# A recurrent mixer whose gate branch runs one block behind its gates, with the gate products in three products of halves

## The reference

```python
def rglru_direction(xc, w_g, b_g, lam, h0, reverse):
    xb = xc.reshape(B, T, LRU_BLOCKS, LRU_BLOCK)              # 8 blocks of 128 channels
    g = jnp.einsum('btnk,gnkj->gbtnj', xb, w_g).reshape(2, B, T, D_RNN) + b_g[:, None, None, :]
    r, ig = jax.nn.sigmoid(g[0]), jax.nn.sigmoid(g[1])
    log_a = -LRU_C * r * jax.nn.softplus(-lam)
    a = jnp.exp(log_a)
    u = jnp.sqrt(-jnp.expm1(2.0 * log_a)) * (ig * xc)
    # h = a * h + u along the tokens, forwards or backwards
def rglru_mixer(...):
    z = h @ w_in                                              # 1024 x 2048
    g, xc = gelu(z[..., :D_RNN]), dwconv_centred(z[..., D_RNN:], conv_w, conv_b)
    y = forward(xc) + backward(xc)                            # two directions
    return (y * g) @ w_out
```

## Time and profile before

| what | value |
|---|---|
| median of 3 runs | 1773.4 us (1772.84 to 1774.81) |
| profiled execution, its own time | 1770.4 us |
| its span in the trace | 1768.7 us |
| mean granted PE clock | 0.985 of full speed |
| PE busy | 1640.8 us (93%) |
| DVE busy | 710.4 us (40%) |
| ACT busy | 553.3 us (31%) |
| POOL busy | 182.1 us (10%) |

### The profile page before, as it was taken

One profiled execution on the slowest core, in us unless ns is written; L12 is line 12 of the kernel. 1 busy time (PEld: TensorE's weight loads), 2 busy tenths in 40 slices (PEclk: granted clock), 3 DMA queues, 4 the chain that ended last, 5 costly groups with the idle time before them and its releaser, 6 DMA issues.

```text
span 1768.7 us, 23506 instructions
## 1 busy us (share of the span) xinstructions
PE 1640.8 (93%) x9838; PEld 876.1 (50%) x9838; DVE 710.4 (40%) x1432; ACT 553.3 (31%) x970; POOL 182.1 (10%) x203
## 2 busy tenths in 40 slices
PE   5999989889999999999989999999969998888887
PEld 3766767543333333333349888888733333222222
DVE  4667666621222122122136766765441222022213
ACT  5777883400111111111027656655300000000002
POOL 1000010010001001001001235433000000000001
PEclk8999999989999999999999999999979999999999
DMA  9555352699999999999993200023499999999996
GB/s 374 199 215 168 121 225 97 238 355 406 393 403 395 391 402 400 390 403 403 396 382 143 72 1 2 1 72 131 188 366 421 420 422 420 422 421 421 421 421 254
DMA packets 89593, 520.78 MB, mean 294 GB/s; under 512 B 11347, under 2 KB 19648, under 8 KB 33936
## 3 DMA queue, kind: packets, MB, share of 16 engines
q1 hardware_dynamic: 80128, 487.74, 68.3%
q0 software_dynamic: 9360, 31.54, 5.7%
HBM read 502.37 MB, written 16.88 MB: 294 GB/s over the span
## 4 chain that ended last, share of the span: by engine, by line
PE 59%; SPq 21%; ACT 7%; DVE 6%; DMA 5%; issue 2%; ACTq 0%; DVEq 0%; POOLq 0%
SPq L576 20%; PE wide L986 14%; PE duo L1041 6%; PE wide L997 6%; PE wide L720 6%; PE turned L650 5%; PE wide L842 4%; PE duo L1053 3%; PE duo L1278 2%; PE wide L1251 2%; DMA sb_ring_x<-moe_w_down 1%; DMA sb_ring<-ada_w 1%; ACT sb_prob L1708 1%; PE wide L1140 1%; DVE sb_asum L2371 1%
## 5 line engine op out<-in xcount | busy, mean ns | idle before, releaser
L986 PE MATMUL wide<-sb_ring_x,sb_xT 128*64 128x512 f32 x1248 | 281.4, 596 | 17.6 <-DMA sb_ring_x<-moe_w_up 16.5
L986 PE MATMUL wide<-sb_ring,sb_xT 128*64 128x512 f32 x800 | 181.4, 596 | 12.3 <-DMA sb_ring<-moe_w_up 12.2
L986 PEld LDWEIGHTS wide<-sb_ring_x,sb_xT 128*64 128x64 f32 x1248 | 85.2, 137 | 195.1 <-issue 146.4
L1041 PE MATMUL duo<-sb_ring_x,sb_hidT 128*64 128x512 f32 x608 | 140.0, 599 | 8.9 <-DMA sb_ring_x<-moe_w_down 8.8
L2065 DVE TENSOR_TENSOR sb_hid<-wide,sb_sg 128x512 f32<-128x512 f32 x16 | 11.1, 692 | 296.5 <-ACT sb_sg_c L1521 296.5
L986 PEld LDWEIGHTS wide<-sb_ring,sb_xT 128*64 128x64 f32 x800 | 54.3, 137 | 127.8 <-issue 93.4
L1519 ACT ACTIVATE sb_sg<-wide 128x512 f32<-128x512 f32 x16 | 9.6, 597 | 324.4 <-PE wide L997 324.4
L2558 POOL TENSOR_TENSOR sb_prob<-sb_prob,sb_asum 128x768 f32<-128x768 f32 x64 | 93.9, 1467 | 149.1 <-DVE sb_asum L2367 149.1
L2065 DVE TENSOR_TENSOR sb_hid<-wide,sb_hid 128x512 f32<-128x512 f32 x16 | 11.1, 692 | 222.8 <-ACT sb_hid L1519 222.8
L1519 ACT ACTIVATE sb_hid<-wide 128x512 f32<-128x512 f32 x16 | 9.6, 597 | 246.8 <-PE wide L986 246.8
L1041 PEld LDWEIGHTS duo<-sb_ring_x,sb_hidT 128*64 128x64 f32 x608 | 40.3, 136 | 93.4 <-issue 72.9
(11 more groups left out here) (479 smaller groups left out, 2881.3 us busy)
## 6 DMA issues: line engine op xcount, KB each, us to landing
sb_ring_x<-moe_w_up SPq DMA_DIRECT2D x156, 1024.0 KB, 28.6
sb_ring<-moe_w_up SPq DMA_DIRECT2D x100, 1024.0 KB, 28.2
sb_ring_x<-moe_w_down SPq DMA_DIRECT2D x79, 1024.0 KB, 27.9
sb_ring<-moe_w_down SPq DMA_DIRECT2D x49, 1024.0 KB, 28.6
sb_ring<-ada_w SPq DMA_DIRECT2D x40, 1024.0 KB, 8.2
sb_ring<-lru_w_in SPq DMA_DIRECT2D x8, 1024.0 KB, 10.1
sb_ring_x<-ada_w SPq DMA_DIRECT2D x8, 1024.0 KB, 25.3
sb_ring<-lru_w_out SPq DMA_DIRECT2D x4, 1024.0 KB, 6.4
```

The lines of the kernel that those rows point to most:

```text
L986: ins = mm(wide[n * CAPL:(n + 1) * CAPL, s, :], mine[:, k, :], w[:, at:at + BANK], start=k == 0, stop=k == KD - 1)
L1041: ins = mm(lat[n * CAPL:(n + 1) * CAPL, :], hidnT[lay][:, 2 * (c % 2) + r, h * CAPL:(h + 1) * CAPL], w[:, r, n * BANK:(n + 1) * BANK], sta ...
```

## The change

Four things change in the mixer.

1. **Order of the projections.** `blocks` begins with u of 0, 1 and 2, and PE runs branch g one block later: in iteration n it does the gates of n, g of n - 1 and u of n + 2. One slice of the contraction (of 8) of g stands between the two gate units; in iteration 0, u of 2 is cut into pieces of 2, 2 and 4 slices around the gates. `in_project` takes the range of slices.
2. **Weight halves.** Those of projection 2n + 1 (g of n - 1) are made after the centring on ACT and after the convolution on DVE. Those of projection 2n + 2 (u of n + 2) are made after the sigmoids on ACT, and on DVE after L1925 (which was L1894).
3. **Gates of halves.** `xc` is split: ACT copies it to `xc_hi` (`rows_hi`), DVE subtracts (`rows_lo`). POOL splits the block's gate weights (`gate_weights`). A gate unit is now twelve fp32r products, six for each gate, at L773.
4. **Gelu.** It goes to a buffer of its own, `gel`, one block behind; DVE writes the sum of directions straight to Y (`s_sum`) and multiplies the block before (`gated`). The special banks of the last projection and unit are gone.

The core of the diff:

```diff
-    blocks = [("u", 0), ("u", 1)]
+    blocks = [("u", 0), ("u", 1), ("u", 2)]
     for n in range(KD):
         blocks.append(("g", n))
-        if n + 2 < KD:
-            blocks.append(("u", n + 2))
+        if n + 3 < KD:
+            blocks.append(("u", n + 3))
...
+        p = at_block["g", n - 1] if n else at_block["u", 2]
         if n == 0:
-            plan += beside + [("gate", n, 0), ("gate", n, 1)]
-        elif n < KD - 1:
-            plan += [("gate", n, 0)] + beside[0:3] + [("gate", n, 1)] + beside[3:]
+            plan += beside + [("in", p, 0, 2), ("gate", n, 0), ("in", p, 2, 4), ("gate", n, 1), ("in", p, 4, KD)]
         else:
-            plan += [("gate", n, 0), ("gate", n, 1)] + beside
-        plan.append(("in", at_block["g", n]))
+            plan += [("gate", n, 0)] + beside[0:3] + [("in", p, 0, 1), ("gate", n, 1)] + beside[3:] + [("in", p, 1, KD)]
         if k1 == KD:
             plan.append(("turn", g))
-        if n + 2 < KD:
-            plan.append(("in", at_block["u", n + 2]))
+        if 0 < n < KD - 2:
+            plan.append(("in", at_block["u", n + 2], 0, KD))
+    plan.append(("in", at_block["g", KD - 1], 0, KD))
...
             def gates(n, d):
 
                 u = 2 * n + d
...
-                pe.wait_ge(s_xc, n + 1)
-                if 1 <= u < 2 * KD - 1:
+                pe.wait_ge(s_setup, NCONST + 4 * n + 4)
+                pe.wait_ge(s_hlo, KD + n + 1)
+                if u:
 
                     pe.wait_ge(s_sig, u)
...
+                for g, lat in enumerate((r_lat, i_lat)):
+                    outs = (lat, ctx_[:, g * TC:(g + 1) * TC])
+                    for i, (w, x_) in enumerate(((w_hi, xc_hi), (w_hi, xc_lo), (w_lo, xc_hi))):
+                        for part in range(2):
+                            ins = mm(outs[part], w[:, g, :], seg(x_, part), start=i == 0, stop=i == 2)
+                ins.then_inc(s_gmm, 1)
...
+            def rows_hi(n):
+
+                act.wait_ge(s_xc, n + 1)
+                if n:
+
+                    act.wait_ge(s_gmm, 2 * n)
+                fn(xc_hi[:], XC[:, n % 2, :], ACT.Copy).then_inc(s_hhi, 1)
+
+            def gelu(n):
+
+                p = at_block["g", n]
+                act.wait_ge(s_z, p + 1)
+                if n:
+
+                    act.wait_ge(s_yg, n)
+                banks = in_banks(p)
+                fn(gel[:, 0:TL], banks[0], ACT.Gelu_apprx_tanh)
+                fn(gel[:, TL:T], banks[1], ACT.Gelu_apprx_tanh).then_inc(s_gelu, 1)
...
+            def rows_lo(n):
+
+                dve.wait_ge(s_hhi, KD + n + 1)
+                v.tensor_tensor(xc_lo[:], XC[:, n % 2, :], xc_hi[:].bitcast(F32), ALU.subtract).then_inc(s_hlo, 1)
+
+            def gated(n):
+
+                dve.wait_ge(s_gelu, n + 1)
+                dve.wait_ge(s_sum, n + 1)
+                v.tensor_tensor(Y[:, n, :], Y[:, n, :], gel[:], ALU.mult).then_inc(s_yg, 1)
...
             for n in range(KD):
                 if n + 1 < KD:
                     convolve(n + 1)
-                if 2 * n + 3 < 2 * KD:
-                    in_lo(2 * n + 3)
+                if n:
+                    in_lo(2 * n + 1)
...
                 if k1 == KD:
                     ada_read(g)
+                if 0 < n < KD - 1:
+                    in_lo(2 * n + 2)
+                if n + 1 < KD:
+                    rows_lo(n + 1)
                 dve.wait_ge(s_ix, 2 * n + 2)
                 scans(n, 0)
                 scans(n, 1)
...
-                if n + 2 < KD:
-                    in_lo(2 * n + 4)
                 h0, h1 = XT[:, 2 * n % 3, :], XT[:, (2 * n + 1) % 3, :]
-                chain.step(v.tensor_tensor(h0, h0, h1, ALU.add))
-                dve.wait_ge(s_gelu, n + 1)
-                v.tensor_tensor(Y[:, n, :], Y[:, n, :], h0, ALU.mult).then_inc(s_yg, 1)
+                v.tensor_tensor(Y[:, n, :], h0, h1, ALU.add).then_inc(s_sum, 1)
+                if n:
+                    gated(n - 1)
+            gated(KD - 1)
...
+            def gate_weights(n):
+
+                for d in range(2):
+                    if n == 0:
+                        pool.wait_ge(landed[place["gate", d][0]], 16 * place["gate", d][1])
+                    elif d == 0:
+
+                        pool.wait_ge(s_gmm, 2 * n)
+                    w, hi, lo = gate_w(n, d)
+                    g_.tensor_copy(hi, w).then_inc(s_setup, 1)
+                    pool.wait_ge(s_setup, NCONST + 4 * n + 2 * d + 1)
+                    g_.tensor_tensor(lo, w, hi.bitcast(F32), ALU.subtract).then_inc(s_setup, 1)
```

More of the change, by code:

```diff
@@ L328, in build @@
         used = [sem(f"used{s}") for s in range(NCH)]
-        s_const, s_parA, s_parB, s_router = [sem(n) for n in ("s_const", "s_parA", "s_parB", "s_router")]
+        s_setup, s_parA, s_parB, s_router = [sem(n) for n in ("s_setup", "s_parA", "s_parB", "s_router")]
         s_partr, s_pcol, s_silu_c = [sem(n) for n in ("s_partr", "s_pcol", "s_silu_c")]
@@ L521, in unit, with gate_w @@
             return 2 * pair + hh, t, pair, hh
+        def gate_w(n, d):
+            slot = place["gate", d][0]
+            pairs = [a[:, slot, :].rearrange("p (g n j) -> p n g j", g=2, j=P)[:, n] for a in (ring, ring_r)]
+            return pairs[0], gw_hi[:, d], pairs[1]
         def in_weights(p):
@@ L736, in first_blocks, with in_project @@
                             ins.then_inc(s_z, 1)
-            def in_project(p, *done):
+            def in_project(p, k0, k1, *done):
                 done = [d for d in done if d is not None]
-                if p == 2 * KD - 1:
-                    pe.wait_ge(s_sig, p)
-                elif p >= 2:
+                if k0 == 0 and p >= 2:
                     kind, n = blocks[p - 2]
                     pe.wait_ge(s_xc if kind == "u" else s_gelu, n + 1)
-                pe.wait_ge(s_wlo, p + 1)
-                for k in range(KD):
+                if k0 == 0:
+                    pe.wait_ge(s_wlo, p + 1)
+                for k in range(k0, k1):
                     ins = in_products(p, k, done)
-                ins.then_inc(s_z, 1)
+                if k1 == KD:
+                    ins.then_inc(s_z, 1)
             def gates(n, d):
                 u = 2 * n + d
-                if n == 0:
-                    arrived(("gate", d))
-                w = ring_at(("gate", d)).rearrange("p (n j) -> p n j", j=P)
-                pe.wait_ge(s_xc, n + 1)
-                if 1 <= u < 2 * KD - 1:
+                _, w_hi, w_lo = gate_w(n, d)
+                pe.wait_ge(s_setup, NCONST + 4 * n + 4)
+                pe.wait_ge(s_hlo, KD + n + 1)
+                if u:
                     pe.wait_ge(s_sig, u)
-                xc = XC[:, n % 2, :]
                 r_lat, ctx_, i_lat = gate_banks(u)
-                mm(r_lat, w[:, n, :], seg(xc, 0), start=True, stop=True)
-                mm(ctx_[:, 0:TC], w[:, n, :], seg(xc, 1), start=True, stop=True)
-                mm(ctx_[:, TC:2 * TC], w[:, KD + n, :], seg(xc, 1), start=True, stop=True)
-                if u == 2 * KD - 1:
-                    pe.wait_ge(s_gelu, KD - 1)
-                mm(i_lat, w[:, KD + n, :], seg(xc, 0), start=True, stop=True).then_inc(s_gmm, 1)
+                for g, lat in enumerate((r_lat, i_lat)):
[4 more added lines that the diff above has]
+                ins.then_inc(s_gmm, 1)
             first_blocks(used[place[plan_chunk(plan[1])][0]])
@@ L1424, in _ @@
                     fn(XT[:, u % 3, :], XT[:, u % 3, :], ACT.Sqrt).then_inc(s_sqrt, 1)
-                p = at_block["g", n]
-                if n + 2 < KD:
-                    in_hi(2 * n + 4)
-                act.wait_ge(s_z, p + 1)
-                banks = in_banks(p)
-                fn(seg(Y[:, n, :], 0), banks[0], ACT.Gelu_apprx_tanh)
-                fn(seg(Y[:, n, :], 1), banks[1], ACT.Gelu_apprx_tanh).then_inc(s_gelu, 1)
+                if n:
+                    gelu(n - 1)
+            gelu(KD - 1)
             def out_weights_hi(lay, *ks):
@@ L2425, in _ @@
-            g_.memset(first[:], float(TL)).then_inc(s_const, 1)
-            pool.wait_ge(s_const, 5)
+                             pattern=[[-1, P]], channel_multiplier=1).then_inc(s_setup, 1)
+            g_.memset(eps[:], EPS).then_inc(s_setup, 1)
+            g_.memset(aff2[:], -1.0).then_inc(s_setup, 1)
+            g_.memset(first[:], float(TL)).then_inc(s_setup, 1)
+            pool.wait_ge(s_setup, 5)
             g_.affine_select(out=first[:], in_=first[:], compare_op=ALU.is_ge, fill=float(TL // 2), base=-2 * E,
-                             pattern=[[0, 1]], channel_multiplier=1).then_inc(s_const, 1)
@@ L2435, in _ @@
[L2435 to L2440 removed]
+                             pattern=[[0, 1]], channel_multiplier=1).then_inc(s_setup, 1)
+            g_.memset(silu_c[:], 0.0).then_inc(s_setup, 1)
@@ L2441, in _ @@
+            g_.memset(idx_t[:], 0).then_inc(s_setup, 1)
+            g_.memset(marks[:], 0.0).then_inc(s_setup, 1)
+            g_.memset(gate_t[:], 0.0).then_inc(s_setup, 1)
```

(15 more changed lines are left out.)

66 lines of the change are left out of this document (29 added, 37 removed).

## The result

The changed kernel takes 1809.58 us (median of 5 runs, 1808.99 to 1812.42), beside 1773.74 (5 runs, 1772.84 to 1774.81) for the one before: ratio 1.0205, 95% interval 1.0194 to 1.0216. The profiled execution took 1808.99 us, with a span of 1807.2.

What follows compares the result with a forecast made beforehand. PE's own work was taken to bound the block (25.45 us). Start 5.5, middle 14.5, end 10.1 and clock 2 make 32 us on the profiled 1770.4: 1802.5, plus 3 for the median, 1805.5 us; range 1790 to 1820.

Steps and rivals of the forecast that it cites:

- Bound and gain: Before, PE's own work sets the 25.45 us block; halves take 0.5 us off a gate unit, about 1.1 a block.
- The two waits: PE waits for DVE's weight rests each middle block: 1 us before branch g's first piece, 3.6 before branch u.
- The clock: One stretch at 1.2 GHz after the start's 8.5 us idle before 97.7: 2 us; none for waits of 3.6 us.
- The second rival: Each block's wait also drops PE's clock: up to 14.7 us more (2.45 each), 1820 us; chance 0.12.
- Start: First blocks: PE idle 5.6 and 8.5 us, so gates of block 2 begin 5.5 us later than 115.69.
- Middle: Blocks 2 to 5: 28.9 us each against 25.45, 4 x 3.45 + 0.7 for a group's addition = 14.5 us.
- End: Blocks 6 and 7 to the output copies: block 7's gelu waits for the one gelu buffer; 10.1 us.
- so it does not add: DVE's scans, sum and old block's product end 1.1 us into the next block, when ACT has just centred.
- The faster rival: Weight rests are in time and PE's saving counts: 24.2 us a block against 25.45, kernel 1768 us; chance 0.05.
- Free parts: POOL's gate weight splits, 2.0 to 5.9 us a block, free at either end; ACT's row copy 0.85 us.
- The signs to look for: Profile after: PE busy in the stage 9 us less, L773 means near 0.34 us, gates every 28.9 us.
- The sum: Whole kernel: 32 us more, 1802.5 us profiled, plus 3 for the median, 1805.5 us; chance 0.75.

Runs made afterwards that it cites:

- e10: Kernel before with gates in halves, its order, weight half and rest of 2n+3 behind the first unit's sigmoids, group reading and start's row subtraction early: 1768.91 us.
- e11: Control for e10: kernel before, fp32 gates and its order, with weight half and rest of 2n+3 behind the first unit's sigmoids and group reading early: 1771.11 us.
- e8: Changed kernel with 12 filler products on PE ahead of each u projection from the fourth block's on: 1806.84 us.
- e6: Changed kernel with the last gelu written to a free buffer and block 6's product between the scans of block 7: 1808.16 us.
- e1: Changed kernel with DVE's weight rest of projection 2n + 2 moved ahead of L1925: 1809.1 us.
- e2: e1 with the high half and rest of projection 2n + 1 also made early, ahead of centring (ACT) and convolution (DVE): 1784.18 us.
- e7: Changed kernel with both rests early, next g's halves made an iteration earlier, block 0's g whole ahead of the second gates, and e6's end: 1780.98 us.
- e12: e10 with filler products: 16 more ahead of the output products, 5 ahead of each of the first mixture's last three modulation chunks: 1764.57 us.

## Why the prediction was right, and where its sizes were off

**Bound and gain.** That PE's work set the block before, and that the halves take 0.5 us off a gate unit, held: a unit takes 2.11 us in halves (139.34 to 141.45 in e10) and 2.58 in fp32 (141.78 to 144.36 in e11).

**The two waits.** Forecast 1 and 3.6 us a block, measured 1.25 and 3.28; the rest for branch u stands behind L1925, as said. Without the fall of the clock the block is 28.8 us (e8), forecast 28.9.

**The clock.** The prediction took one cold stretch at the start (2 us) and none for the waits of 3.6 us "at the edge". That is the term that was mis-sized. Four projections took 10.15 to 10.25 us, 6.6 us together, and the stretch behind 97.65 cost 2.7 (8.13 us from there to ACT's next weight half, in the block after it 5.41): 9.3 us on the path, not 2. A stretch behind the wait ahead of block 7's gates is not on the chain, which runs over ACT there. The second rival came in part, in four blocks and with 1.65 us instead of 2.45, since a stretch lasted 3.4 us and not 4.9. The Trainium skill, page "TensorE: Matmul & The Clock Gate", section "HAM oscillation", describes gaps that throttle the clock in each turn of a loop; this trace agrees for the waits of 3.28 us, while those of 1.25 us, which come in each turn too, were not followed by a fall.

**Start.** Forecast 5.5 + 2 for the clock = 7.5 us; gates of block 2 begin at 123.59 instead of 115.69, 7.9 later, of which the clock is 2.7 and the order 5.2. The gates at 84.00 and the piece at 97.65 came within 0.1 us of the forecast 84.1 and 97.7.

**Middle.** Forecast 14.5 us, measured 19.8: gates of block 6 at 245.48, 27.7 after those of before, less the start's 7.9. These began at 217.75; the 217.5 of the prediction was worked out from blocks of 25.45 and not read. Four cold stretches are 6.6, the steps were 1.0 shorter than forecast, and before took 0.3 longer than it was given.

**End.** Forecast 10.1, measured 37.7 - 27.7 = 10.0. The cause, "only then is the one gelu buffer free", is in the trace, but it is the smaller part: with a buffer of its own (e6) the end is 1.2 us shorter, and then PE's last projection holds the gelu.

**DVE "so it does not add".** True as long as the wait for branch u stands, and no longer: e1 showed a ring of 28.3 us through the same DVE work, just behind the one of 28.8. The faster rival's price (24.2 a block if the rests are in time) was right for PE, but it takes more than both rests early: with these the block is 24.9 (e2), and only with the further moves of e7 24.08.

**Free parts.** POOL's splits were taken as 2.0 to 5.9 us a block; they take 0.40 and 0.74 us, twice, 2.3 in all (3.0 in the block at 225), and nobody waits for them. ACT's copy, taken as 0.85, takes 0.73 of ACT's time.

**The signs to look for.** PE's busy time in the stage was to fall by 9 us. It rose by 6.1 (203.40 in 55 to 300, before 197.29 in 55 to 264): a pair of products takes 0.64 us at 1.2 GHz (145.34 to 145.98) instead of 0.354, so a busy time says little where the clock moves. The mean of the L773 groups, forecast near 0.34, is 0.30 for 256 columns and 0.43 for 512; it is the pair's pitch that is 0.354.

**The sum.** Forecast 32, measured 37.7 in the stage and 38.5 in the span. The clock is 7.3 us more than forecast, the other terms 1.7 less. The prediction added 3 us from the profiled execution to the median; here that step is 0.6 (1808.99 to 1809.58). So the median was missed by 4.1 us and the profiled execution by 6.5; the difference of 2.4 is luck. What sets where a cold stretch falls from run to run stays open: in e12 two more came, at the first gates (66 and 73 us), and cost 3.0 us.

## What to carry to other kernels

When one step is moved past another on an engine that waits, lay out all the rings of a loop (chains of waits that come back to their own start) with their lengths, not only the longest: the second here was 0.5 us shorter, and undoing the first alone won nothing. An engine that is 93% busy is set back by any step that others do for it too late; put such steps (weight halves, readings) where their engine waits anyway. And when a stage becomes shorter, look at the waits that grow behind it: filler products there, on top of the halves, gave 4.3 us (from 1768.91 to 1764.57), the halves themselves 2.2.
